# A modulation vector taken as row sums on VectorE instead of weighted sums on VectorE and column sums on TensorE

## What is computed

```python
mod = jax.nn.silu(c) @ w_ada[l] + b_ada[l]            # (1, 1024) @ (1024, 6144)
sh1, sc1, gt1, sh2, sc2, gt2 = [m[:, None, :] for m in jnp.split(mod, 6, axis=-1)]
h = rmsnorm_2(x, norm1_w[l]) * (1.0 + sc1) + sh1
x = x + gt1 * hybrid_mixer(h, ...)
h2 = rmsnorm_2(x, norm2_w[l]) * (1.0 + sc2) + sh2
x = x + gt2 * expert_choice_ffn(h2, ...)
```

## Time and profile before

| what | value |
|---|---|
| runs | 1741.92, 1736.0, 1741.11 us; median 1741.11 |
| profiled execution | 1736.3 us, span 1734.5 us |
| mean granted TensorE clock | 0.938 of full speed |
| busy share of the span | PE 88%, DVE 35%, ACT 15%, POOL 2% |
| HBM traffic | 391.31 MB read, 227 GB/s over the span |

### The profile page before, as it was taken

How to read it: one execution, slowest core, us unless ns; L and a number is a source line. 1 busy time by engine, 2 the same in 40 slices (tenths; PEclk the granted TensorE clock), 3 DMA queues, 4 the chain that set the end, 5 groups by cost and what they waited for, 6 DMA issues and landing times.

```text
span 1734.5 us, 20947 instructions
## 1 busy us (share of the span) xinstructions
PE 1534.3 (88%) x9040; PEld 1158.4 (67%) x9040; DVE 612.1 (35%) x1311; ACT 261.1 (15%) x622; POOL 30.2 (2%) x52
## 2 busy tenths in 40 slices
PE   9999999999999999999998999999967565666665
PEld 7878888888877788888887888768853221121211
DVE  4536215347524541253565727733230000000000
ACT  1231021000112411210001222232021000000000
POOL 0000000000010000000000012000000000000000
PEclk9999999999999999999999899999979998877877
DMA  9515415765434154266654003332849999999997
GB/s 376 203 68 194 145 59 232 287 256 185 145 135 146 34 209 146 96 224 262 243 182 146 1 1 108 111 99 98 346 193 429 428 430 428 429 429 428 428 429 325
DMA packets 42828, 395.29 MB, mean 228 GB/s; under 512 B 15856, under 2 KB 18288, under 8 KB 19056
## 3 DMA queue, kind: packets, MB, share of 16 engines
q1 hardware_dynamic: 42032, 392.46, 57.4%
q0 software_dynamic: 272, 1.05, 0.2%
q10 hardware_dynamic: 432, 0.44, 0.1%
HBM read 391.31 MB, written 2.62 MB: 227 GB/s over the span
## 4 chain that ended last, share of the span: by engine, by line
PE 73%; DMA 23%; DVE 2%; issue 1%; ACT 0%; SPq 0%; DVEq 0%; ACTq 0%
PE pb L450 51%; DMA ring<-in_w_experts 22%; PE pb L897 11%; PE pb L548 7%; PE pb L832 3%; DMA inverses_turned<-arena 1%; PE pb L617 1%; PE pb L772 0%; PE pb L1199 0%; PE pb L675 0%; ACT arena L1374 0%; DVE rstd L1738 0%; PE pb L1206 0%; PE pb L910 0%; DVE arena L1998 0%
## 5 line engine op out<-in xcount | busy, mean ns | idle before, releaser
L450 PE MATMUL pb<-hT,ring 128*128 128x256 f32 x2176 | 484.2, 382 | 0.0
L450 PEld LDWEIGHTS pb<-hT,ring 128*128 128x128 f32 x2176 | 412.8, 191 | 62.1 <-issue 7.6
L2417 DVE SCALAR_TENSOR_TENSOR side<-side,pb 128x256 f32<-128x256 f32 x16 | 6.7, 421 | 410.2 <-ACT side L1374 410.2
L1374 ACT ACTIVATE arena<-pb 128x512 f32<-128x512 f32 (+4 forms) x162 | 74.3, 472 | 508.7 <-PE pb L450 393.2
L450 PE MATMUL pb<-ring,hT 128*32 128x512 f32 (+2 forms) x512 | 96.5, 674 | 43.7 <-DMA ring<-in_w_experts 42.3
L548 PE MATMUL pb<-arena,ring 128*128 128x256 f32 x512 | 118.2, 382 | 0.0
L450 PE MATMUL pb<-arena 128*64 128x128 f32 (+5 forms) x592 | 93.0, 441 | 19.8 <-DMA arena<-in_w_experts 15.1
L450 PE MATMUL pb<-ring,arena 128*32 128x512 f32 (+1 forms) x416 | 68.0, 766 | 44.3 <-DMA ring<-in_w_experts 44.3
L548 PEld LDWEIGHTS pb<-arena,ring 128*128 128x128 f32 x512 | 95.2, 190 | 14.5 <-issue 2.9
L450 PEld LDWEIGHTS pb<-ring,hT 128*32 128x32 f32 (+1 forms) x512 | 34.1, 147 | 94.0 <-DMA ring<-in_w_experts 50.9
L450 PEld LDWEIGHTS pb<-arena 128*64 128x64 f32 (+3 forms) x592 | 55.0, 164 | 56.6 <-issue 26.9
(11 more groups left out here) (326 smaller groups left out, 1737.1 us busy)
## 6 DMA issues: line engine op xcount, KB each, us to landing
ring<-in_w_dense SPq DMA_DIRECT2D x86, 2048.0 KB, 8.1
ring<-in_w_experts SPq DMA_DIRECT2D x72, 2048.0 KB, 36.0
arena<-in_w_experts SPq DMA_DIRECT2D x24, 2048.0 KB, 35.6
ring<-in_w_dense SPq DMA_DIRECT2D x2, 1536.0 KB, 7.5
cons<-in_cons SPq DMA_DIRECT2D x1, 1808.0 KB, 18.1
xT<-in_xT SPq DMA_DIRECT2D x1, 1024.0 KB, 6.1
side<-in_memT POOLq DMA_DIRECT2D x1, 1024.0 KB, 6.3
out<-xT SPq DMA_DIRECT2D x4, 256.0 KB, 2.2
```

The lines of the kernel that those rows point to most:

```text
L450: return nc.tensor.matmul(o, l, r, start=st, stop=sp)
L1374: return nc.scalar.activation(o, i, f, **kw)
L2417: V.scalar_tensor_tensor(tg[:, e % 2, :], tg[:, e % 2, :], 1.0, ps[:, 0:S], ALU.add, ALU.mult).then_inc(eg_ready, 1)
```

## The change

The modulation is computed from the transposed weights. A unit now holds 512 output features by 1024 inputs: feature on the partition, four groups of 128 features, 1024 inputs along the free axis. A row of silu(c) of 1024 values is broadcast to all partitions (`c_row`), and one `tensor_tensor_reduce` over 128x1024 multiplies and sums a group, starting from `b_ada`, directly into one column of `modc`. The product itself is written over the weights in the ring slot. There are four such instructions for a unit, 24 for a layer, spread over n = 0 to 13 of the loop: one for n = 0, 3, 7 and 10, two for the ten others, none for n = 14 and 15. PE's `modulation` and DVE's `modulated` are gone.

To make the row, SP stores `csil` to HBM ahead of the load of unit 8 and waits for that store; later it loads the row with a broadcast into 128 partitions (512 KB written), once for each layer, right behind the load that reuses the slot of that layer's second value unit (unit 10 in layer 0). DVE waits for the row (`c_row_in`) at the first unit of each layer. The weights are transposed on the host, outside the measured time.

```diff
-ADA_TURN = (2, 3, 4, 6, 7, 8)
-ADA_DONE = (6, 8, 10, 14, 16, 16)
...
-                unit(a["w_ada_2"], 0, D, 512 * (len(ada_units) - 1), 512)
+                unit(a["w_ada_T"], 512 * (len(ada_units) - 1), 512, 0, D)
...
-        ada_acc = view(arena, 8192, 4, 512)
+        c_row = view(arena, 11264, D)
...
+        c_d = nc.dram_tensor("c_silu_row", (P, DC), F32).ap()
...
-            def modulation(i):
-
-                pe.wait_ge(ada_ready, i + 1)
-                ps = fill(f"ada{i}", 4)
-                for f in range(4):
-                    last = mm(ps[:, f:f + 1], ada_acc[:, i % 4, f * P:(f + 1) * P], ones[:, 0:1], True, True)
-                mark(last, f"ada{i}")
...
-                    if i in ADA_TURN:
-                        modulation(6 * layer + ADA_TURN.index(i))
...
-                    if i == 0:
-                        modulation(6 * layer + 5)
...
+                if u == 8:
+                    sp.wait_ge(c_ready, 1)
+                    sp.dma_start(c_d, csil).then_inc(c_stored, 16)
+                    sp.wait_ge(c_stored, 16)
...
                 sp.dma_start(t[:, at:at + n], w[:, 0:n]).then_inc(loaded[slot_of[u]], 16)
+                if before in (value_unit[0, 1], value_unit[1, 1]):
+                    sp.dma_start(c_row, c_d.rearrange("p k -> (p k)").unsqueeze(0).broadcast_to([P, D])).then_inc(c_row_in, 16)
...
-            def weigh_modulation(i, k):
+            def weigh_modulation(i, f):
 
                 u = [v for v in ada_units if ada_units[v] == i][0]
-                w, acc = slot_ap(u)[:, k, :], ada_acc[:, i % 4, :]
-                if k == 0:
-                    if i == 0:
-                        dve.wait_ge(c_ready, 1)
+                w = slot_ap(u)[:, f, :]
+                if f == 0:
+                    if i % 6 == 0:
+                        dve.wait_ge(c_row_in, 16 * (i // 6 + 1))
                     dve.wait_ge(loaded[slot_of[u]], 16 * nth[u])
-                    link(V.tensor_scalar(acc, w, csil[:, 0:1], None, ALU.mult))
-                    return
-                ins = V.scalar_tensor_tensor(acc, w, csil[:, k:k + 1], acc, ALU.mult, ALU.add)
-                if k < DC - 1:
-                    link(ins)
-                else:
+                ins = V.tensor_tensor_reduce(out=w, in0=w, in1=c_row, scale=1.0, scalar=col("b_ada", 4 * i + f), op0=ALU.mult,
+                                             op1=ALU.add, accum_out=modc[:, 4 * i + f:4 * i + f + 1])
+                if f == 3:
                     ins.then_inc(ada_ready, 1)
-
-            def modulated(i):
-
-                ps, free = full(dve, f"ada{i}")
-                V.tensor_tensor(modc[:, 4 * i:4 * i + 4], ps[:, 0:4], col("b_ada", 4 * i, 4), ALU.add).then_inc(free, 1)
...
-                    for j in range(6):
-                        if ADA_DONE[j] == n:
-                            modulated(6 * layer + j)
-                    for o in range(3 * n, 3 * n + 3):
-                        weigh_modulation(6 * layer + o // 8, o % 8)
-                modulated(6 * layer + 4)
+                    for o in range(12 * n // 7, min(12 * (n + 1) // 7, 24)):
+                        weigh_modulation(6 * layer + o // 4, o % 4)
                 prepare(layer, 0)
-                modulated(6 * layer + 5)
                 prepare(layer, 1)
                 if layer:
-                    copied(dve, *(f"ada{i}" for i in range(12)))
+                    dve.wait_ge(ada_ready, 12)
```

More of the change, by code:

```diff
@@ L329, in program @@
         hid_ready = sem("mlp_squared")
-        c_tanh, c_ready, ada_ready = sem("c_tanh"), sem("c_silu"), sem("modulation_rows_summed")
+        c_tanh, c_ready, ada_ready = sem("c_tanh"), sem("c_silu"), sem("modulation_summed")
+        c_stored, c_row_in = sem("c_stored"), sem("c_row_loaded")
         cin_ready, cv_ready, cvt_ready, cvs_ready = sem("conv_in"), sem("convolved"), sem("conv_tanh"), sem("conv_silu")
@@ L2486 @@
         axis=1).reshape(NE * 6, P, UNIT)
-    weights = {name: a[name][0] for name in ("ab_w_in", "ab_w_out", "cd_w_in", "cd_w_out", "w_ada_2", "w_in_2",
+    weights = {name: a[name][0] for name in ("ab_w_in", "ab_w_out", "cd_w_in", "cd_w_out", "w_in_2",
                                              "w_attn_up_2", "w_dn_up_2", "w_o_2")}
     weights |= {name: a[name] for name in ("xa_w_q", "xa_w_kv", "xa_w_o", "mlp_w_up", "mlp_w_down")}
+    weights["w_ada_T"] = a["w_ada_2"][0].T.reshape(-1, DC, P).transpose(0, 2, 1).reshape(-1, D)
     weights["cd_w_kv"] = grouped(a["cd_w_in"][0][:, 2048:2304])
```

## The result

Over five runs of each, the ratio of the changed kernel to the one before is 0.9923, with a 95% interval of [0.9907, 0.9939]: 13.4 us faster on 1740.8. The medians are 1724.6 us (1723.76 to 1730.95) and 1740.76 us (1736.0 to 1741.92). The forecast, 1730.7 us and a ratio of 0.9940, has the right sign and lies just outside that interval: 3 us of the gain are not in its sum. In absolute time the changed kernel's median lies 6.1 us under the forecast and only 0.1 us above the lower end of its range, 1724.5. The profiled execution took 1724.6 us with a span of 1722.8, 11.7 us less than before.

A forecast was written before the change was run, and what follows sets the result against it. PE was taken to bound the MLPs and DMA the experts' part, which moves forward with PE. Savings of 3.56 + 1.66 = 5.22 us a layer, 10.4 for both, gave 1741.1 - 10.4 = 1730.7 us, range 1724.5 to 1738.

The forecast's parts named there:

- Blocks on PE: Removed 128x1 matmuls cost PE 0.89 us a block; four in each up phase give 3.56 us a layer.
- The seam block: Block after up unit 7, before the down units: PE would idle those 1.10 us anyway, so 0 gained, at most 0.89.
- The stall in down unit 0: PE's third down product waits for `prepare`, late behind DVE passes; 0.77 us a layer goes, with its block 1.66.
- DVE covered: 48 reductions of 1.35 us with the read, 65 us in all, stay hidden behind PE's half units of 6.9 us.
- The bound at 3.6 us: Reductions averaging above 3.6 us make DVE set the MLP's pace; rival of a far slower reduction, chance 0.03.
- SP's queue: The `csil` store ahead of unit 8 takes up to 10.3 us, hidden by 17.3 us of cover; row loads cost 0.
- The gain reaches the end: The DMA-bound experts' part moves forward with PE, first load about 10 us sooner; rival, not passed on, 1741, chance 0.07.
- The clock at the seam: Rival: PE's 1.1 us idle between up and down units lowers its clock, 5 us at each seam, 1740.7; chance 0.08.

The follow-up runs named there:

- block_seam: The changed kernel with only the block of four 128x1 matmuls after up unit 7 put back in each layer; ratio to before 0.9963, mean 1733.9 us.
- last_banks: The changed kernel with both half units of up unit 7 put into PSUM banks 6 and 7; ratio to before 0.9917, mean 1725.8 us.
- before_spread14: The kernel before with its 48 DVE passes a layer spread over n = 0 to 13 instead of 0 to 15; ratio 1.0005, mean 1739.6 us.
- spread16: The changed kernel with its 24 reductions a layer spread over n = 0 to 15 instead of 0 to 13; ratio to before 0.9935, mean 1728.5 us.
- blocks_all: The changed kernel with six blocks of four 128x1 matmuls put back on PE in each layer, on constant operands; ratio to before 0.9995, mean 1739.4 us.
- front2: The changed kernel with two blocks of four 128x1 matmuls in PE's idle time at about 13 us; ratio to before 0.9965, mean 1733.7 us.

## Why the prediction was right, and where it was short

- **Blocks on PE**, 0.89 us each and not their duration of 240 ns: right. The up phase is 3.62 us shorter (forecast 3.56), and putting the blocks back costs 4.45 for five.
- **The seam block gives nothing**: right, by block_seam; last_banks shows that what PE waits for there is the last ReLU's bank.
- **The stall in down unit 0**, 0.77 us: right. It goes with the blocks still in (before_spread14, 0.74) and comes back in spread16 (0.80). Each MLP got 5.19 us shorter where 5.22 was forecast.
- **DVE covered**: right. 1276 ns was forecast at 1271, with the read 81. The rule of the Trainium skill ("Vector Engine (DVE) Microarchitecture Reference", "Points that are easy to get wrong") is that the scalar-tensor-tensor shape runs at half throughput from two non-bf16 sources in SBUF. It is not borne out for this operation: 1276 ns lies on the slope of the rows with one source in PSUM, where the estimate by the rule was 2.4 us. The profile lists it as CUSTOM_DVE_ANT_0, and whether it has the page's shape isn't shown. The bound at 3.6 us held from both sides, at 2.6 and at 3.9.
- **SP's queue** covered: right, the store took 8.5 us of the 17. The row's loads, priced at 1.2 us each by their bytes, landed after 9.1, which is covered too.
- **The gain reaches the end**: right, 11.5 us at the first experts' load, of which 10.4 are the MLPs'; 0.5 were there before the first MLP, in the start, and the rest came in the stages between. The experts' part did keep its length: from its first piece of 9.07 us to the end of the span it is 447.9 us before and 447.7 after.
- **The clock at the seam** stayed up. The row from 365 to 375 us of the changed kernel:

```profile
365.00:375.00 10.00, 9.10 (x43) 7.72 (x42) 4.49 (x6) 0.63 (x1) 0.00 (x0) 1.00 0.72 262
```

What the sum lacks is a term for a stage that the change doesn't touch. It adds the MLPs' gain to the whole time, as if everything between the second MLP and the experts kept its length, but that late stage takes 142 to 153 us, by the waits and the clock in it, and PE's instructions ahead of it matter. Where both traces have a short late stage, as the first two do, the spans differ by 11.7 us: 10.4 in the MLPs, 0.5 in the start, 0.5 in the late stage, and 0.3 elsewhere. The mean of 11 runs of the changed kernel is 12.3 us under that of 27 of before (1739.9), 1.9 more than the 10.4. By what share of the runs had the long late stage the mean can move by some us, and this share isn't measured closely for either kernel; the surplus may be no more than that. That blocks_all lies 2.8 us over what its MLPs explain is no second proof, since it is compared with the same eleven runs. So the remainder isn't shown to belong to the change.

The median of 1724.6 us owes its distance from the forecast to luck: three of its five runs were of the faster group. Over all eleven runs the mean is 1727.6, 3 us under the 1730.7 forecast.

What PE waits for in the burst is open too: the profile names no releaser, and the supply of instructions is a guess.

## What to carry to other kernels

To price an instruction on the engine that sets the pace, read the starts around it, and then look at what ends the wait next to it: of six equal blocks five were worth 0.89 us and one nothing. Work on a covered engine is free until its total, with what it must do besides, reaches the pace, and what stands last before a handover counts at once. With a change of half a per cent, compare the stages that it touches in the trace: the MLPs repeated to 0.01 us where whole runs differed by 10. And look for a stage that has two lengths in one and the same kernel before a difference of means is put down to the change.

## What the runs showed of the hardware

- With eight small matmul instructions some 1100 us ahead, in idle time, a kernel was 6 us slower in the mean (front2, 5 runs): longer waits and a lower clock in and behind a burst of 32x32 matmuls. One kernel, unchanged, had that stage at 143.3 and at 149.2 us in two executions.
- In the repetition of the changed kernel the granted clock was 1.00 from 1167.30 to 1172.30 us with PE busy throughout, and 0.64 in the 6.70 us behind it; in the first trace it stayed 1.00 there.
- After an idle time of 0.90 us 16 records of matmuls took 3.69 us at a granted clock of 1.00, after 4.40 us 5.10 at 0.72, and after 23.56 us 6.74 at 0.55, near twice: almost throughout the lower of the two clock levels (1.2 instead of 2.4 GHz).
- A store of 4 KB issued 0.4 us behind a load of 2 MB on the same queue landed after 8.5 us; the loads of 2 MB have a median of 8.3 us from issue to landing.
